# Two chunks of the first projection as seven products each, with the sums of tokens and weights made by GpSimd

## The reference

```python
def rms_norm(x, g):
    y = xf * lax.rsqrt(jnp.mean(xf * xf, axis=-1, keepdims=True) + NORM_EPS) * g

n = rms_norm(h, norm_mix[l])
proj = n @ w_in
q_r, fz_f, fz_b, i_r, g_r, q_a, k_a, v_a, gate_r, gate_a = jnp.split(proj, SPLIT_IDX, axis=-1)
qh = jax.nn.silu(q_r) * (HG_KEY_DIM ** -0.5)
f = lb + (1.0 - lb) * jax.nn.sigmoid(z)          # z is fz_f or fz_b, 512 columns each
```

## Time and profile before

| | us |
|---|---|
| median of three runs | 2682.22 |
| the profiled execution, its own time | 2681.49 |
| its span, from the first to the last instruction | 2679.7 |
| PE busy | 2673.7 |
| DVE busy | 2159.0 |
| ACT busy | 1091.9 |
| POOL busy | 472.6 |

### The profile page before, as it was taken

How to read it: one execution, slowest core, us unless ns; L and a number is a source line. 1 busy time by engine, 2 the same in 40 slices (tenths; PEclk the granted TensorE clock), 3 DMA queues, 4 the chain that set the end, 5 groups by cost and what they waited for, 6 DMA issues and landing times.

```text
span 2679.7 us, 39638 instructions
## 1 busy us (share of the span) xinstructions
PE 2673.7 (100%) x16144; PEld 2366.9 (88%) x16144; DVE 2159.0 (81%) x2181; ACT 1091.9 (41%) x1200; POOL 472.6 (18%) x292
## 2 busy tenths in 40 slices
PE   9999999999999999999999999999999999999999
PEld 7978789888999889999777899998999989899998
DVE  6778866569999889888586988879887888798885
ACT  4433634444444463333363533335333342343332
POOL 0124124041000341001234100022000130410000
PEclk9999999999999999999999999999999999999999
DMA  4221133222222322323311222232322233222232
GB/s 172 82 77 63 51 110 141 95 79 94 97 110 101 121 94 95 111 95 112 116 48 63 95 107 99 100 121 95 111 95 106 101 110 110 95 95 100 106 108 97
DMA packets 39910, 266.29 MB, mean 99 GB/s; under 512 B 4544, under 2 KB 5824, under 8 KB 8512
## 3 DMA queue, kind: packets, MB, share of 16 engines
q1 hardware_dynamic: 38160, 259.02, 27.2%
q10 hardware_dynamic: 1584, 4.87, 0.5%
HBM read 261.77 MB, written 2.10 MB: 98 GB/s over the span
## 4 chain that ended last, share of the span: by engine, by line
PE 99%; DVE 1%; issue 0%; DMA 0%; ACT 0%; SPq 0%; DVEq 0%; ACTq 0%
PE ps L2239 31%; PE ps L2240 31%; PE ps L2241 31%; PE ps L2503 1%; PE ps L2917 1%; PE ps L2583 1%; PE ps L2525 1%; PE ps L2624 0%; PE ps L2957 0%; PE ps L2930 0%; PE ps L2597 0%; PE ps L2513 0%; PE ps L2285 0%; DVE h L1295 0%; PE ps L2794 0%
## 5 line engine op out<-in xcount | busy, mean ns | idle before, releaser
L568 ACT ACTIVATE w_hi<-stage 128x2048 fp32r<-128x2048 f32 (+1 forms) x241 | 410.2, 1702 | 448.6 <-PE ps L2241 439.9
L2239 PE MATMUL ps<-x_hi,w_hi 128*128 128x256 f32 (+1 forms) x1624 | 559.0, 344 | 0.7 <-DVE w_lo L1349 0.6
L2241 PE MATMUL ps<-x_hi,w_lo 128*128 128x256 f32 (+1 forms) x1624 | 549.9, 339 | 0.0
L2240 PE MATMUL ps<-x_lo,w_hi 128*128 128x256 f32 (+1 forms) x1624 | 549.8, 339 | 0.0
L1139 DVE TENSOR_TENSOR w_lo<-stage,w_hi 128x2048 fp32r<-128x2048 f32 (+1 forms) x240 | 492.8, 2053 | 44.7 <-ACT w_hi L568 41.1
L2239 PE MATMUL ps<-f_hi,w_hi 128*128 128x512 f32 x880 | 342.9, 390 | 0.0
L2240 PE MATMUL ps<-f_lo,w_hi 128*128 128x512 f32 x880 | 342.9, 390 | 0.0
L2104 POOL TENSOR_TENSOR up_b<-up_b,gate_b 128x1024 f32<-128x1024 f32 x50 | 113.4, 2268 | 1300.8 <-PE ps L2241 1212.3
L2241 PE MATMUL ps<-f_hi,w_lo 128*128 128x512 f32 x880 | 342.3, 389 | 0.0
L2239 PEld LDWEIGHTS ps<-x_hi,w_hi 128*128 128x128 f32 x1624 | 308.3, 190 | 36.2 <-issue 3.1
L2240 PEld LDWEIGHTS ps<-x_lo,w_hi 128*128 128x128 f32 x1624 | 308.4, 190 | 34.6 <-issue 3.1
(11 more groups left out here) (486 smaller groups left out, 5172.5 us busy)
## 6 DMA issues: line engine op xcount, KB each, us to landing
stage<-in_stream SPq DMA_DIRECT2D x241, 1024.0 KB, 4.8
h<-in_x ACTq DMA_DIRECT2D x2, 1024.0 KB, 5.5
out_x<-h SPq DMA_DIRECT2D x8, 256.0 KB, 2.0
h<-in_x SPq DMA_DIRECT2D x6, 256.0 KB, 3.8
mem_raw<-in_mem ACTq DMA_DIRECT2D x1, 1024.0 KB, 4.7
stage<-in_stream SPq DMA_DIRECT2D x6, 128.0 KB, 4.0
stage<-in_stream SPq DMA_DIRECT2D x1, 640.0 KB, 7.8
h<-in_x SPq DMA_DIRECT2D x1, 512.0 KB, 6.2
```

The source lines that it names most:

```text
L568: act.activation(w_hi[slot][:, 0:width], stage[slot][:, 0:width], ACT.Copy).then_inc(hi_ready, 1)
L2239: pe.matmul(out_ap, wh, xh, start=first, stop=False)
L2240: pe.matmul(out_ap, wh, xl, start=False, stop=False)
L2241: return pe.matmul(out_ap, wl, xh, start=False, stop=last)
```

## The change

The fourth and the sixth chunk are stored in the stream as quarters and are computed by `seven_products`, in banks 4 to 7, in a new order for the kind "query": the two products that use the chunk alone, then the four with weight sums, then the one with a token sum. Scaled tokens come into a new buffer, half by ACT and half by DVE. POOL makes the four token sums and, for each of the two chunks, the four weight sums. The low part of the fourth chunk moves on DVE from ahead of `norm_rstd` to behind it and behind two of the four `t_lo`. The loops `qf_step` of ACT and DVE are written out. The rotary angles stand ahead of the taking out of the sixth chunk instead of behind it.

```diff
--- before.py
+++ after.py
@@ -67,6 +67,7 @@
 CONV_SEVENS = [4, 6, 8, 10]
+FIRST_SEVENS = [3, 5]
@@ -200,6 +201,8 @@
+        tx_first = place("tx_first", hid(4), [P, KT, S])
+        sf_hi, sf_lo = place("sf_hi", hid(12), [P, 4 * KP * P], F32R), place("sf_lo", TMP, [P, 4 * KP * P], F32R)
@@ -432,7 +438,7 @@
         def four_banks(i, p):
 
-            if i == "c_in":
+            if i in ("qf", "c_in"):
                 return 4
@@ -596,8 +602,9 @@
             def tokens_scaled(i):
 
-                for k in range(KT):
-                    act.activation(t_x[:, k, :], h[:, k, :], ACT.Copy, scale=pc(GAIN[i], k)).then_inc(t_scaled, 1)
+                scaled = tx_first if i == "qf" else t_x
+                for k in range(KP if i == "qf" else KT):
+                    act.activation(scaled[:, k, :], h[:, k, :], ACT.Copy, scale=pc(GAIN[i], k)).then_inc(t_scaled, 1)
@@ -713,7 +720,9 @@
             c0 = C0["qf"]
+            tokens_scaled("qf")
             split_hi((c0 + 2, 0))
+            split_hi((c0 + 3, 0), SINGLES)
             act.wait_ge(both_gain, 2)
             act.activation(pc("root", 0, 8), pc("root", 0, 8), ACT.Sqrt, bias=pc("eps", 0)).then_inc(both_gain, 1)
             stat(0)
@@ -722,11 +731,19 @@
-            def qf_step(it):
-                split_hi((c0 + 3, it * 2))
-                split_hi((c0 + 4, it * 2))
-
-            walk(act, 2, qf_step)
+            def first_sums_hi(p):
+
+                act.wait_ge(s_sum, 4 * NTH["qf", p] + 4)
+                act.activation(sf_hi[:, :], s_f[:, :], ACT.Copy).then_inc(s_rounded, 1)
+
+            sums_rounded("qf")
+            first_sums_hi(3)
+            split_hi((c0 + 4, 0))
+            first_product("qf", 3)
+            split_hi((c0 + 5, 0), SINGLES)
+            first_sums_hi(5)
+            split_hi((c0 + 6, 0))
+            first_product("qf", 5)
             split_hi((c0 + 7, 0))
@@ -1369,6 +1386,8 @@
+            for k in range(KP, KT):
+                dve.tensor_scalar(tx_first[:, k, :], h[:, k, :], pc("norm_mix", k), None, ALU.mult).then_inc(t_scaled, 1)
             raw_queries(0)
@@ -1394,8 +1413,32 @@
             raw_queries(1)
-            split_lo((c0 + 3, 0))
             norm_rstd(0)
+
+            def query_rest(p):
+
+                n = NTH["qf", p]
+                dve.wait_ge(s_sum, 4 * n + 4)
+                split_lo((c0 + p, 0), SINGLES)
+                dve.wait_ge(s_rounded, n + 1)
+                dve.tensor_tensor(sf_lo[:, :], s_f[:, :], sf_hi[:, :].bitcast(F32), ALU.subtract).then_inc(s_ready, 1)
+
+            def queries(j):
+
+                dve.wait_ge(chunk_done, c0 + j + 1)
+                if j in FIRST_SEVENS:
+                    evacuated("qf", j, qf[:, 2 * j:2 * j + 2, :])
+                else:
+                    for e in range(2):
+                        dve.tensor_tensor(qf[:, 2 * j + e, :], ps[:, (t0 + 2 * j + e) % 4, :], rstd[:, :], ALU.mult).then_inc(acc_evac, 1)
+
+            token_lo("qf", 0)
+            token_lo("qf", 1)
+            query_rest(3)
+            token_lo("qf", 2)
+            token_lo("qf", 3)
+            queries(2)
+            split_lo((c0 + 4, 0))
@@ -1403,16 +1446,12 @@
-            def qf_step(it):
-                for j in range(2):
-                    dve.wait_ge(chunk_done, it * 2 + (c0 + j + 1))
-                    for e in range(2):
-                        dve.tensor_tensor(row(qf, it * 4 + 2 * j + e), ps[:, (t0 + 2 * j + e) % 4, :], rstd[:, :], ALU.mult).then_inc(acc_evac, 1)
-                    split_lo((c0 + j + 2, it * 2))
-
-            walk(dve, 3, qf_step, 1)
-
+            queries(3)
+            query_rest(5)
+            queries(4)
+            split_lo((c0 + 6, 0))
+
+            dve.wait_ge(s_ready, len(FIRST_SEVENS))
             dve.tensor_tensor(r_diag[:, :, :], rstd[:, :].rearrange("p (a n) -> p a n", a=BLK), free(ident, 0, [[0, BLK], [1, P]]),
                               ALU.mult).then_inc(r_col_step, 1)
@@ -1439,6 +1478,8 @@
+            queries(5)
+            split_lo((c0 + 7, 0))
@@ -2106,6 +2147,37 @@
+            def first_token_sums():
+
+                x11, x12 = tx_first[:, 0:KP, 0:HALF], tx_first[:, 0:KP, HALF:S]
+                x21, x22 = tx_first[:, KP:KT, 0:HALF], tx_first[:, KP:KT, HALF:S]
+                pool.wait_ge(t_scaled, KT)
+                pool.tensor_tensor(t_f[:, T1, :, :], x12, x11, ALU.subtract).then_inc(t_sum, 1)
+                pool.wait_ge(t_sum, 1)
+                pool.tensor_tensor(t_f[:, T2, :, :], x22, t_f[:, T1, :, :], ALU.subtract).then_inc(t_sum, 1)
+                pool.wait_ge(t_sum, 2)
+                pool.tensor_tensor(t_f[:, T3, :, :], t_f[:, T2, :, :], x11, ALU.subtract).then_inc(t_sum, 1)
+                pool.tensor_tensor(t_f[:, T4, :, :], x21, t_f[:, T2, :, :], ALU.subtract).then_inc(t_sum, 1)
+
+            def first_weight_sums(p):
+
+                c, n, w = C0["qf"] + p, NTH["qf", p], KP * P
+                a11, a12, a22, a21 = (stage[c % 2][:, w * q:w * q + w] for q in range(4))
+                s1, s2, s3, s4 = (s_f[:, w * q:w * q + w] for q in range(4))
+                pool.wait_ge(landed[c % 2], 16 * (c // 2 + c % 2))
+                if n:
+                    pool.wait_ge(s_ready, n)
+                pool.tensor_tensor(s1, a21, a22, ALU.add).then_inc(s_sum, 1)
+                pool.tensor_tensor(s3, a11, a21, ALU.subtract).then_inc(s_sum, 1)
+                pool.wait_ge(s_sum, 4 * n + 1)
+                pool.tensor_tensor(s2, s1, a11, ALU.subtract).then_inc(s_sum, 1)
+                pool.wait_ge(s_sum, 4 * n + 3)
+                pool.tensor_tensor(s4, a12, s2, ALU.subtract).then_inc(s_sum, 1)
+
+            first_token_sums()
+            first_weight_sums(3)
+            first_weight_sums(5)
             pool.wait_ge(f_ready1, 8)
@@ -2372,6 +2444,8 @@
                 product(2, single(1, 0), tokens(1, 0)).then_inc(first_done, 1)
+                if kind == "query":
+                    with_sums()
                 pe.wait_ge(t_ready, 4 * TOKENS[i] + 4)
                 mm = product(4, single(1, 1), token_sum(T4))
@@ -2455,7 +2529,11 @@
             for j in range(3, 6):
-                plain(C0["qf"] + j, T0["qf"] + 2 * j, x)
+                if j in FIRST_SEVENS:
+                    pe.wait_ge(std_ready, 1)
+                    seven_products("qf", j, "query")
+                else:
+                    plain(C0["qf"] + j, T0["qf"] + 2 * j, x)
@@ -3076,7 +3154,7 @@
-    out = _pairs(q_r) + _pairs(f_heads) + _pairs(i_r)
+    out = _pairs(q_r) + [(_quarters if c + 2 in FIRST_SEVENS else _pairs)(f_heads)[c] for c in range(4)] + _pairs(i_r)
```

More of the change, by code:

```diff
@@ L386, in cc @@
             return const_in[:, CCOL[name]:CCOL[name] + n]
-        GAIN = {0: "norm_ffn", 1: "both", 2: "ffn2_0", 3: "ffn1_1", "c_in": "mix_1", 4: "ffn2_1"}
+        GAIN = {"qf": "norm_mix", 0: "norm_ffn", 1: "both", 2: "ffn2_0", 3: "ffn1_1", "c_in": "mix_1", 4: "ffn2_1"}
         FOLLOWED = {
@@ L406, in build @@
         SEVEN_ORDER[before_last:before_last] = [("c_in", p) for p in CONV_SEVENS]
+        SEVEN_ORDER[0:0] = [("qf", p) for p in FIRST_SEVENS]
         NTH = {at: n for n, at in enumerate(SEVEN_ORDER)}
-        S_FIRST = {at: n for n, at in enumerate((i, p) for i, p in SEVEN_ORDER if i != "c_in" and ORDER[p][0] == "gate")}
-        TOKENS = {0: 0, 1: 1, 2: 2, 3: 3, "c_in": 4, 4: 5}
+        S_FIRST = {at: n for n, at in enumerate((i, p) for i, p in SEVEN_ORDER if i not in ("qf", "c_in") and ORDER[p][0] == "gate")}
+        TOKENS = {"qf": 0, 0: 1, 1: 2, 2: 3, 3: 4, "c_in": 5, 4: 6}
         def summed_at(i, p):
+            if i == "qf":
+                return sf_hi, sf_lo
             if i == "c_in":
@@ L417, in chunk_at @@
         def chunk_at(i, p):
-            if i == "c_in":
-                return C0["c_in"] + p, T0["c_in"] + 2 * p
+            if i in ("qf", "c_in"):
+                return C0[i] + p, T0[i] + 2 * p
             return C0[f"up{i}"] + p, T0[f"up{i}"] + TILE_AT[p]
```

## The result

The kernel after takes 2689.52 us (median of 7 runs, 2689.30 to 2692.13), the kernel before 2681.86 on the same chips (7 runs, 2681.72 to 2682.74). The ratio is 1.0031, 95% interval 1.0021 to 1.0041: 0.31% slower by the means of the runs and 0.29% by the medians, against 2689.2 and 0.26% forecast. The profiled execution took 2689.43 with a span of 2687.6, 7.9 more than the 2679.7 of before. All medians here leave out three runs that took 8% or more longer than the others of their kernel (one of experiment 6, two of the kernel before).

The account below looks back on a forecast made before the run. PE, busy 2673.7 of 2679.7 us, was taken to bound the kernel. 2.5 + 2.55 + 3.5 - 1.6 gave +7.0 us (6.95): 2688.4 on the profiled execution, 2689.2 on the median, 0.26% slower; range 2680.6 to 2692.0.

Parts of the forecast that it names:

- take turns: POOL operations and DVE operations with two SBUF operands never run at once; when one ends, the other engine's waiting one goes.
- Rival 1: POOL and DVE don't meet, or turns fall kindly: third chunk's low part by 28.6, time 2680.7; chance 0.14.
- rival 2: DVE keeps its turn while it has work ready: third low part at 29.3, +1.7, 2683.9; chance 0.18 with half-way orders.
- First wait: PE ahead of its third chunk, whose low part on DVE is delayed by POOL's sums: 2.5 us lost.
- Second wait: PE inside the third chunk, ahead of the sum over features, with `x_ss` late at 36.45: 2.55 us lost.
- Third wait: PE ahead of the fourth chunk, whose low part DVE delivers at 49.2 instead of 45.65: 3.5 us lost.
- the clock at 0: PE's granted clock falling to 1.2 GHz behind waits: taken as 0, with 1.8 us kept for the upper end.
- PEclk under 9 in the first slice: Sign in the profile's granted-clock row that would speak for the clock part of Rival 3.
- Gain on PE: Fourth and sixth chunks as seven products take 10.08 us each instead of 10.88: 1.6 us saved.
- The later covers: Work after the fourth chunk's start stays hidden from PE: 0 us, thinnest at the sixth chunk with 0.7 to spare.
- Rival 3: Late covers break too: 2 us at the sixth chunk and 1.8 of clock, 2693; chance 0.08.
- rival 4: Seven products run at the rate of eight, so no gain on PE: +1.6 us; no separate chance given.

Follow-up runs that it names:

- experiment 6: Changed kernel with only the sixth chunk as seven products, the fourth plain again, POOL's sums held back and token parts later: 2680.87 us, ratio 0.9997 to the kernel before.
- experiment 1: Changed kernel with POOL's twelve sums each cut to 16 columns, the rest filled with zeros: 2680.31 us, ratio 0.9994 to the kernel before.
- experiment 5: Changed kernel with POOL's sums replaced by memsets of the same tiles: 2680.26 us, ratio 0.9994 to the kernel before.
- experiment 4: Changed kernel with POOL's first token sum held back until DVE has ended its small operations: 2690.39 us, ratio 1.0031 to the kernel before.
- experiment 2: Kernel before with only the token scaling and POOL's four token sums added, results unused, all chunks plain: 2689.31 us, ratio 1.0027 to the kernel before.
- experiment 3: Changed kernel with 22 unread matmuls, eleven ahead of the third chunk and eleven ahead of the matmul over `ssum`: 2691.12 us, ratio 1.0034 to the kernel before.
- experiment 7: Changed kernel with the rotary angles behind the evacuation of the sixth chunk again: 2689.72 us, ratio 1.0031 to the kernel before.
- experiment 8: Changed kernel with the 22 unread matmuls, and DVE's reciprocal moved behind all four `t_lo` and the fourth chunk's low part: 2690.16 us, ratio 1.003 to the kernel before.

## Why the prediction was right, point by point

- **That POOL and DVE take turns, and that this decides.** Shown: experiments 1 and 5 take away the meetings (and with them POOL's length, which experiment 4 shows to be a bound of its own when POOL starts later), and 9.2 us go; experiment 2 puts four sums in alone, on which nothing waits, and most of the loss comes; in the kernel after DVE is full (21.86 of 22), so it does not stand waiting for POOL's results. Rival 1 (no meetings) and rival 2 (DVE keeps its turn) did not happen here: the low part of the third chunk ended at 31.89, not 28.6 or 29.3.
- **First wait, 2.5.** Measured 3.0, and PE came 0.29 later. POOL's first sum took 2.40 alone, not the 2.00 of the earlier trace rows, and the second ended 2.25 after DVE, not 1.87. The row of the price had plain tiles; these sums take halves of every tile, which may be why. That was not tried.
- **Second wait, 2.55.** Measured 3.32 (`ssum` at 37.97 instead of 36.45): four POOL sums, each 0.32 to 0.39 more than taken.
- **Third wait, 3.5, and the clock at 0.** This split failed: the wait was 0.37, and 2.9 us of lower clock stood in its place. The prediction had put the clock's cost at 0 with up to 1.8 on top of the sum; it should have seen that a delay inside the third chunk is hidden as long as the fourth waits for DVE. Experiments 3 and 7 show this: with the clock full, or low elsewhere, the fourth chunk starts at 50.23 and 50.73 instead of 50.40. The right term was never three waits, but one time: that of DVE's low part, forecast at 49.2 and measured at 50.30. DVE was 1.5 late on the forecast at `ssum`, by the four POOL sums, and 1.1 at the reciprocal (42.90 for 41.8) and at the low part, since the small operations and copies between took 0.4 less than taken. The sign that the prediction named for the clock, PEclk under 9 in the first slice, could not show it: even 3.5 us at half clock in a slice of 67 us leave 0.97.
- **Gain on PE, 1.6.** Measured 1.5, in the kernel after and in experiment 1: 0.73 from the fourth chunk and 0.81 from the sixth, less 0.03 at the fifth.
- **The later covers, at nothing.** Held. The low parts of the fifth and sixth chunks were ready at 58.73 (forecast near 57.6) and 70.42 (69.5), PE came to them at 60.55 and 71.46. The thinnest kept 1.0 us, since PE was late as well. The angles stood from 75.94 to 84.3, the low part behind them was ready at 90.45 for 93.05; experiment 7 shows them free. Rival 3 with a break at the sixth chunk did not happen, nor did rival 4.
- **The sum.** 50.40 less 40.45 less 1.5 is 8.45 at 93 us, where the forecast had 6.95; measured in the spans 7.9 and in the medians 7.66. At 93 us the sum was thus 1.5 too small: 1.2 by the later start of the fourth chunk (1.1 of it DVE's chain), 0.1 by the gain, and 0.2 by the start of the fourth chunk before, which the sum took at 40.65. That is ACT's row for the end of the third chunk; PE's own row is at 40.45, so the third chunk took 11.8 and not the 12.0 or 11.9 of the prediction. Of the 1.5, 0.5 came back in the later shrinking, which no step had foreseen, and 0.3 since the profiled execution of before (2681.49) lay further under its median than that of after. The forecast of the time came within 0.3 us since, besides, the median it stood on (2682.22) was 0.36 above that of the seven runs. So the mechanism held, and the last microsecond did by luck.

What stays open: why one instruction of DVE near 289 us came 0.35 later in the profile of before than in all the others; what sets the clock's fall, which came behind the first wait, the second, the wait for the fourth chunk, or that for the fifth, in kernels that differ little. Seven runs of the kernel after spread over 2.8 us and those of before over 1.0; the two slowest of after (2691.87 and 2692.13) have a mean clock of 0.998, the other five 0.999, those of before 1.000. That the spread is the clock fits this, but where it fell in each run was not shown.

## What to carry to other kernels

An engine that stands idle is not free to use while another works through the same access to SBUF: price a GpSimd sum of two SBUF tiles as nearly its own duration taken out of VectorE's time (here 2.0 to 2.2 us for each sum of 2.40), and use it where VectorE, not only GpSimd, has slack (the sixth chunk had it, the fourth did not). Its own length is a second bound: held back, the eight sums came too late by themselves. Where several waits lie on one engine's chain, work out when that chain delivers to the last of them, not the sum of the waits: everything in between, a lower clock too, hides under it. Work that keeps the array busy or moves an operation back on a full engine only changes where the wait stands.

## What the runs showed of the hardware that was not expected

- The width of an instruction hardly matters to how long it waits for its turn: a POOL sum of 16 columns, 0.22 us alone, took 4.50 in experiment 1. It stood behind two of DVE's instructions of 2.28 that followed each other at once (the rows below), so the turns are not strict: as at 618.73 in the earlier trace rows, DVE can keep its turn. What the other engine loses does go by the width: DVE's two took 2.28 each, as alone.

```profile
47.09 4.50 POOL L2179 TENSOR_TENSOR s_f<-stage,s_f 128x16 f32<-128x16 f32 x1
...
46.99 2.28 DVE L1156 TENSOR_TENSOR w_lo<-stage,w_hi 128x2048 fp32r<-128x2048 f32 x1
49.19 2.28 DVE L1443 TENSOR_TENSOR qf<-qf,rstd 128x2048 f32<-128x2048 f32 x1
```

- POOL's memset of 1024 columns (0.96) and DVE's addition (2.28) ran at once without loss to either.
- Behind a wait of 2.2 us (2.00 of it idle by the row), after a chunk at full clock, the granted clock fell to its lower level (experiment 8); behind one of 9.0 (experiment 4) the matmuls were slow from the first on, with the windows at 0.86 and 0.91. The Trainium skill says in "TensorE: Matmul & The Clock Gate", Part 1, that an idle array falls back to 1.2 GHz. The traces agree: matmuls of 512 columns 0.43 apart instead of 0.227, those of 256 columns 0.213 instead of 0.12 (experiment 3).
